# Filter taps of two layers side by side on TensorE, GpSimd's stores moved, own buffers for layer 1's filter pieces

## The reference, cut to what matters

```
hid = sin(freq1 * (z @ w1 + b1))              # z: (256, 33) positions
hid = sin(freq2 * (hid @ w2 + b2))            # (256, 64)
h = (hid @ w3).reshape(256, 2, 512)           # the taps, forward and backward
h = h * exp(-t * abs(decay))                  # the envelope
l1 = sum(abs(h_fwd)) + sum(abs(h_bwd[1:]))    # per channel
filt = concat(h_fwd, 0, reversed h_bwd[1:]) / l1
y = irfft(rfft(u) * rfft(filt))
```

## Time and profile before

| | us |
|---|---|
| median of three runs | 1394.13 |
| lowest, highest | 1393.94, 1396.18 |
| the profiled execution, whole | 1395.68 |
| its span, first to last instruction | 1393.9 |
| PE busy in it | 1356.5 (97%) |
| DVE busy | 780.2 (56%) |
| ACT busy | 547.8 (39%) |
| POOL busy | 193.1 (14%) |

### The profile page before, as it was taken

The page is one execution under the profiler, slowest core; times in us unless marked ns, Lnnn a source line. Parts: engine busy times, 40 slices in busy tenths (PEclk is TensorE's granted clock), DMA queues, the critical chain, the costliest instruction groups (busy, mean ns, idle before and its releaser), DMA issues.

```text
span 1393.9 us, 19649 instructions
## 1 busy us (share of the span) xinstructions
PE 1356.5 (97%) x8084; PEld 1111.0 (80%) x8084; DVE 780.2 (56%) x1127; ACT 547.8 (39%) x847; POOL 193.1 (14%) x179
## 2 busy tenths in 40 slices
PE   7999999999999999999999999999999999999997
PEld 3557756777777887877778888888769999899996
DVE  5555575234548676544223443376866788765663
ACT  5652373332233323433112331244555444553552
POOL 1251000603100152000000002200004404100012
PEclk9999999999999999999999999999999999999999
DMA  9333303444631363345443335324325647455561
GB/s 374 130 108 112 116 1 121 159 166 141 219 124 46 131 246 122 105 148 173 149 152 106 106 105 213 136 81 140 107 75 177 226 137 275 149 189 190 182 195 63
DMA packets 55289, 205.28 MB, mean 147 GB/s; under 512 B 6261, under 2 KB 6645, under 8 KB 53664
## 3 DMA queue, kind: packets, MB, share of 16 engines
q1 hardware_dynamic: 52992, 194.22, 40.1%
q0 software_dynamic: 2208, 9.81, 1.9%
HBM read 200.86 MB, written 3.15 MB: 146 GB/s over the span
## 4 chain that ended last, share of the span: by engine, by line
PE 90%; DVE 4%; ACT 2%; POOL 2%; issue 1%; DMA 1%; SPq 0%; DVEq 0%; ACTq 0%
PE ps L1548 27%; PE ps L1550 26%; PE ps L1549 26%; PE ps L1849 2%; PE ps L1577 2%; PE ps L1860 1%; PE ps L1873 1%; DMA pairs<-in_pairs 1%; PE ps L1945 1%; PE ps L1957 1%; DVE wl L1033 1%; PE ps L1805 1%; PE ps L1602 0%; DVE rstd L1071 0%; ACT wh L720 0%
## 5 line engine op out<-in xcount | busy, mean ns | idle before, releaser
L1548 PE MATMUL ps<-xh,wh 128*128 128x512 f32 (+2 forms) x1392 | 473.3, 340 | 2.7 <-DVE xl L1100 1.4
L1033 DVE TENSOR_TENSOR wl<-raw,wh 128x1024 fp32r<-128x1024 f32 (+2 forms) x272 | 353.8, 1303 | 218.0 <-ACT wh L720 214.9
L1549 PE MATMUL ps<-xl,wh 128*128 128x512 f32 (+2 forms) x1392 | 466.4, 335 | 0.0
L1550 PE MATMUL ps<-xh,wl 128*128 128x512 f32 (+2 forms) x1392 | 466.0, 335 | 0.0
L720 ACT ACTIVATE wh<-raw 128x1024 fp32r<-128x1024 f32 (+2 forms) x272 | 283.6, 1043 | 321.0 <-PE ps L1550 320.2
L1548 PEld LDWEIGHTS ps<-xh,wh 128*128 128x128 f32 (+1 forms) x1392 | 260.4, 187 | 45.2 <-issue 14.3
L1550 PEld LDWEIGHTS ps<-xh,wl 128*128 128x128 f32 (+1 forms) x1392 | 260.6, 187 | 29.1
L1549 PEld LDWEIGHTS ps<-xl,wh 128*128 128x128 f32 (+1 forms) x1392 | 261.5, 188 | 27.9 <-issue 1.0
L1548 PE MATMUL ps<-hid_h,wh 128*128 128x512 f32 (+1 forms) x512 | 172.5, 337 | 0.0
L1549 PE MATMUL ps<-hid_l,wh 128*128 128x512 f32 (+1 forms) x512 | 171.7, 335 | 0.0
L1550 PE MATMUL ps<-hid_h,wl 128*128 128x512 f32 (+1 forms) x512 | 171.6, 335 | 0.0
(11 more groups left out here) (246 smaller groups left out, 1442.9 us busy)
## 6 DMA issues: line engine op xcount, KB each, us to landing
raw<-in_units SPq DMA_DIRECT2D x262, 512.0 KB, 3.3
mod_ring<-in_mod_units SPq DMA_DIRECT2D x49, 512.0 KB, 4.0
gap_hy<-in_mod_units SPq DMA_DIRECT2D x15, 512.0 KB, 5.5
pairs<-in_pairs SPq DMA_DIRECT2D x6, 1024.0 KB, 14.3
gap_relu<-in_mod_units SPq DMA_DIRECT2D x7, 512.0 KB, 4.6
raw<-in_units SPq DMA_DIRECT2D x6, 384.0 KB, 2.9
h<-in_x SPq DMA_DIRECT2D x4, 512.0 KB, 7.9
mod_ring<-in_pairs SPq DMA_DIRECT2D x2, 1024.0 KB, 14.6
```

The source lines that it names most:

```text
L1033: dve.tensor_tensor(wl[:, g % SLOTS, 0:n], raw[:, g % SLOTS, 0:n], wh[:, g % SLOTS, 0:n].bitcast(F), ALU.subtract)\
L1548: pe.matmul(dst, w_h, m_h, start=first, stop=False)
L1549: pe.matmul(dst, w_h, m_l, start=False, stop=False)
L1550: return pe.matmul(dst, w_l, m_h, start=False, stop=last)
```

## The change

- A tap now is two matmuls, one after the other: layer 0's from partitions 0 to 63 into bank 7 and layer 1's from 64 to 127 into bank 6. There are four of these, in wave steps 3 to 6, and none behind the wave. Each waits until both results of the one before are weighted.
- VectorE weights both results, and so needs both envelopes from step 4 on. Its four weightings behind the wave are gone.
- ScalarE makes layer 0's envelope in step 1 instead of 3 and layer 1's in step 4 instead of 6.
- GpSimd's order becomes parts(0), abs_sum(0), parts(1), save(0), abs_sum(1), save(1).
- Layer 1's pieces go to tiles that are free by then (`decay`, `filt_top`, `f_w3`); their copies no longer wait for stores. One semaphore per layer counts the stores, where layer 0 had four.
- TensorE waits for all eight weightings before the first spectrum, since spectra use banks 7 and 6, and later spectra wait for the copy two before in every case.

```diff
+            filt_top = alloc(s, "filt_top", (HY,))
+            filt_out = [[filt0[:, i * HY:(i + 1) * HY] for i in range(4)],
+                        [decay[:, 0:HY], decay[:, HY:], filt_top[:, :], f_w3[:, 0:HY]]]
...
             def filter_parts(f):
                 for tb in range(2):
-                    pool.wait_ge(f_weighted, 4 * f + 2 * tb + 2)
+                    pool.wait_ge(f_weighted, 4 * tb + 3 + f)
...
-                    pool.dma_start(filt_scratch[f, :, i * HY:(i + 1) * HY], filt0[:, i * HY:(i + 1) * HY]).then_inc(f_saved[f][i], 16)
+                    pool.dma_start(filt_scratch[f, :, i * HY:(i + 1) * HY], filt_out[f][i]).then_inc(f_saved[f], 16)
...
             filter_abs_sum(0)
+            filter_parts(1)
             filter_save(0)
-            filter_parts(1)
             filter_abs_sum(1)
...
             def filter_copy(f, i):
-                if f:
-                    act.wait_ge(f_saved[0][i], 16)
                 act.wait_ge(f_spec, 4 * f + i + 1)
-                act.activation(filt0[:, i * HY:(i + 1) * HY], ps[:, 7 - i % 2, :], ACT.Copy).then_inc(f_copied, 1)
+                act.activation(filt_out[f][i], ps[:, 7 - i % 2, :], ACT.Copy).then_inc(f_copied, 1)
...
                 if m == 2:
                     filter_sines(1)
-                elif m == 3:
+                elif m == 1:
                     filter_envelope(0)
-                elif m == 6:
+                elif m == 4:
                     filter_envelope(1)
...
             def filter_weighted(i):
-                f, tb, d = i // 4, i // 2 % 2, i % 2
-                if i % 4 == 0:
+                tb, d = divmod(i, 2)
+                dve.wait_ge(f_taps, i + 1)
+                for f in range(DEPTH):
                     dve.wait_ge(f_env, 2 * f + 2)
-                dve.wait_ge(f_taps, i + 1)
-                src = ps[:, 7 - i % 2, :]
+                    src = ps[:, 7 - f, :]
...
                     latent(i, WAVE_BANKS[i])
-                    for i in range(4, 8):
-                        filter_weighted(i)
                     latent(WAVE, KV1_BANK)
...
             def filter_taps(i):
-                f, tb, d = i // 4, i // 2 % 2, i % 2
-                rows = slice(f * HIDDEN, (f + 1) * HIDDEN)
-                if i >= 2:
-                    pe.wait_ge(f_weighted, i - 1)
-                if i in (4, 5):
-                    pe.wait_ge(f_copied, i - 1)
-                pe.matmul(ps[:, 7 - i % 2, :], f_hid2[rows, tb * 128:(tb + 1) * 128],
-                          f_w3[rows, d * HY:(d + 1) * HY], start=True, stop=True).then_inc(f_taps, 1)
+                tb, d = divmod(i, 2)
+                if i:
+                    pe.wait_ge(f_weighted, 2 * i)
+                for f in range(DEPTH):
+                    rows = slice(f * HIDDEN, (f + 1) * HIDDEN)
+                    mm = pe.matmul(ps[:, 7 - f, :], f_hid2[rows, tb * 128:(tb + 1) * 128],
+                                   f_w3[rows, d * HY:(d + 1) * HY], start=True, stop=True)
+                mm.then_inc(f_taps, 1)
...
             pe.wait_ge(ftab_in_s, 16)
+            pe.wait_ge(f_weighted, 8)
             for i in range(2):
                 filter_spectrum(0, i)
             first_kv()
             for i in range(2, 4):
                 filter_spectrum(0, i)
-            for i in range(4, 8):
-                filter_taps(i)
             key_pe(0)
```

More of the change, by code:

```diff
@@ L425, in backbone @@
         f_env, f_parts, f_abs, f_summed = (sem(n) for n in ("f_env", "f_parts", "f_abs", "f_summed"))
-        f_saved = [sems("f_saved_0", 4), sems("f_saved_1", 1) * 4]
+        f_saved = sems("f_saved")
         f_taps, f_weighted, f_l1, f_l1_ready = sem("f_taps"), sem("f_weighted"), sem("f_l1"), sem("f_l1_ready")
@@ L683, in _ @@
                 pool.wait_ge(y_added[layer], KB)
-                for i in range(4):
-                    pool.wait_ge(f_saved[layer][i], 64 if layer else 16)
+                pool.wait_ge(f_saved[layer], 64)
                 pool.dma_start(ftab[:, :, :], fwd_in).then_inc(tables_loaded, 16)
@@ L1145, in filter_weighted @@
             def filter_weighted(i):
-                f, tb, d = i // 4, i // 2 % 2, i % 2
-                if i % 4 == 0:
+                tb, d = divmod(i, 2)
+                dve.wait_ge(f_taps, i + 1)
+                for f in range(DEPTH):
                     dve.wait_ge(f_env, 2 * f + 2)
-                dve.wait_ge(f_taps, i + 1)
-                e = envelope[:, f, tb, d * HY:(d + 1) * HY]
-                src = ps[:, 7 - i % 2, :]
[L1153 to L1156, removed]
+                    e = envelope[:, f, tb, d * HY:(d + 1) * HY]
+                    src = ps[:, 7 - f, :]
+                    if d:
+                        dve.scalar_tensor_tensor(e, src, not_first[:, tb:tb + 1], e, ALU.mult, ALU.mult).then_inc(f_weighted, 1)
+                    else:
+                        dve.tensor_tensor(e, src, e, ALU.mult).then_inc(f_weighted, 1)
             def filter_l1(f):
@@ L1245, in _ @@
                 if layer == 0:
-                    for i in range(4):
-                        dve.wait_ge(f_saved[DEPTH - 1][i], 64)
+                    for f in range(DEPTH):
+                        dve.wait_ge(f_saved[f], 64)
                 dve.wait_ge(kpe_rotated, layer + 1)
@@ L1693, in filter_spectrum @@
                     pe.wait_ge(f_parts, 4 * f + 4)
-                if i >= 2:
+                if o >= 2:
                     pe.wait_ge(f_copied, o - 1)
```

## The result

The changed kernel takes 1399.56 us (median of 8 runs, 1396.37 to 1401.07) against 1394.26 us for the kernel before (8 runs, 1393.81 to 1396.73): ratio 1.0029, 95% interval 1.0020 to 1.0038. By the medians it is slower by 5.3 us (their quotient is 1.0038), by the recorded ratio by 4.0 us (2.8 to 5.3); 1.0 was forecast, and 1399.56 lies outside the range. The profiled execution took 1401.05 us (span 1399.2).

A forecast was written before the change was run, and what follows sets the result against it. TensorE was taken to bound the wave, GpSimd's chain the stretch behind it up to the last column sums. 0.93 + 0 + 0 + 4 x 0.01 = +1.0 us on 1394.13 gave 1395.1 us, range 1393.0 to 1397.9.

The forecast's parts named there:

- First envelope, +0.93: Wave step 1: the envelope on ScalarE, no longer covered by a tap, delays step 2's matmuls by 0.93 us.
- Taps, 4 x 0.01: Four wave slots: two taps on different row halves run together, adding 0.00 to 0.03 us a slot.
- Rival A: Tap slots: the halves do not run together, each slot grows by 0.82 us, 1398.4 us in all; chance 0.10.
- The four late taps "go", worth nothing: Behind the wave: removing at least 3.3 us of TensorE taps gains nothing, since they lie beside GpSimd's chain.
- Table loads, second envelope, decay: Wave on ScalarE: two added 1.28 us loads, the second envelope at step 4 and its decay load are covered; cost 0.
- D: ScalarE: each table switch takes 1.4 us more than its 1.28, +3.5 us, 1397.7 us; chance 0.02.
- B: Wave: layer 1's decay load lands late; at 13 us it costs 2.6 more, 1397.7 us; chance 0.05.
- GpSimd, 16.8 us: GpSimd's chain to the end of layer 1's sums keeps its 16.8 us; cost 0, the 0.93 passed on.
- C: GpSimd's adds are less disturbed by VectorE's weight remainders, 1.6 us go, 1393.4 us; chance 0.13.
- E: GpSimd: with all four stores behind all sums, 2.19 us would go, 1392.8 us; no separate chance given.
- anything else slower: Catch-all for slower outcomes not named among the forecast's cases; no size, chance 0.02.

The follow-up runs named there:

- fill_end: Changed kernel plus three products of zeros on TensorE ahead of the last column sums; 1394.83 us, ratio 1.0002 to the kernel before.
- env_moved: Kernel before with only the envelopes moved, to wave steps 1 and 4; 1394.90 us, ratio 1.0007 to the kernel before.
- late_fill: Changed kernel plus four products of zeros on TensorE where the four late taps stood; 1395.63 us, ratio 1.0018 to the kernel before.
- stores_last: Changed kernel with all GpSimd stores behind both layers' sums; 1394.18 us, ratio 1.0001 to the kernel before.
- parts_first: Changed kernel with GpSimd's order both layers' parts, then both sums, then stores; 1391.14 us, ratio 0.9979 to the kernel before.
- parts_same_half: Changed kernel with GpSimd doing parts, sums, then stores, and both taps on partitions 0 to 63, layer 1's filter not computed; 1394.64 us, ratio 1.0000.
- env34: Changed kernel with envelopes in wave steps 3 and 4 and an own, early loaded decay tile for layer 1; 1397.44 us, ratio 1.0022.
- b_order: Kernel before with the change's own buffers and GpSimd order, taps as before; 1395.88 us, ratio 1.0007 to the kernel before.
- fill_both: Changed kernel plus three products of zeros ahead of the last column sums and two ahead of wave step 2's turn; 1396.91 us, ratio 1.0017.

## Why the prediction was wrong, point by point

- **First envelope, +0.93.** Right as a stall: six kernels with the envelope in step 1 and no filler there have 30.28 to 30.34 us for the wave against 29.37, so +0.91 to +0.97 (fill_end, env_moved, late_fill, stores_last, parts_first; parts_same_half 32.89 - 3 x 0.85 = 30.34). In the two traces of the change the stall was longer (1.60 and 1.56 instead of 0.85 to 0.88) because ScalarE's copy in step 1 came later against TensorE: at 30.98 and 30.72, where stores_last has 30.09, with the turn at 31.58, 31.37 and 31.46. The addition that leads to it stood behind VectorE's three weight remainders and began at 28.87 and 28.61, against 27.57. Behind the longer stall the clock fell: 5.63 - 4.09 = 1.54 us more. The forecast had no term for that. The late addition goes back to an earlier fall, at 12 to 14 us, before the first instruction that the change moved. The rows are the changed kernel's, then stores_last's:

```profile
12.00:14.00 2.00, 2.00 (x4) 0.86 (x3) 1.97 (x5) 1.86 (x4) 1.06 (x2) 0.50 0.99 412
13.56 4.30 PE L1713 MATMUL ps<-normed,consts 128*128 128x512 f32 x8
12.00:14.00 2.00, 2.00 (x6) 0.73 (x5) 1.97 (x5) 1.98 (x3) 1.06 (x2) 1.00 0.98 410
12.72 3.60 PE L1713 MATMUL ps<-normed,consts 128*128 128x512 f32 x8
```

These eight products end at 17.86 against 16.32, and VectorE's reciprocal, which waits for ScalarE behind them, starts at 18.62 (18.36 in the other trace of the change) against 17.08. Of the fourteen traces only one more, env34's, has the early fall; its addition is late as well (29.02), but no envelope stands in its step 1, and its wave is the old 29.40. Why the early fall came in both traces of the change and in none of the seven other kernels with the envelope in step 1 isn't settled. The change's own eight runs spread over 4.7 us: the five from 1398.76 up have mean clocks of 0.991 to 0.993, the three below 0.994 and 0.995.
- **Taps, 4 x 0.01.** Right: 1.13 us a slot with four instructions, 1.12 before. Rival A is refuted, by the change's trace and by parts_same_half.
- **The four late taps "go", worth nothing.** This is the step that failed most. Their absence saved nothing, as the prediction said, since GpSimd was the bound. But they had also kept TensorE at work until GpSimd was done: its spectra ended at 87.08 + 3.83 = 90.91 and the last sum at 90.98. The prediction itself foresaw "TensorE then waiting for GpSimd ahead of the last column sums" and priced that wait at 0. It was 2.59 us long, and behind it the column sums took 1.72 instead of 1.05 and the sums of squares 7.01 instead of 4.56: 0.67 + 2.45 = 3.1 us on the path. fill_end takes these 3.1 us off this stretch. The taps aren't the only thing that held the gap shut: b_order has all taps and waits 0.96 us, because its parts are late.
- **Table loads, second envelope, decay.** Right, 0. Two loads of 1.28 us were added, and a sine or exponential starts 0.01 to 0.02 us behind a load; D falls. The second absolute value at 47.22 follows the copy at 46.94 directly, without waiting for its load; B falls.
- **GpSimd, 16.8 us.** Right: 76.34 to 91.97 + 1.26 = 93.23, 16.9 us. C's gain didn't come: the last add is down to 1.26 from 2.13, but the two before it are up to 3.63 from 2.63, a remainder of VectorE beside other adds now. The wave's shift is passed on 1:1 here too: from slot 4 to the first sum it is 12.14 us in both traces.
- **E.** The order was read rightly, and stores_last shows what it withholds. The estimate of -2.2 us for it was right for that stretch (34.74 against 36.92). It was reckoned against a kernel without a fall; against the change as it ran, the stretch became 5.43 us shorter.

By size: the steady stretch was forecast at 99.93. From the forecast to 104.37 there are 0.39 us of earlier start (first product of step 2 at 38.23, not 38.62), 1.58 from there to slot 4 (25.97 against 24.39, nearly all the slow step 2), 0.13 of GpSimd's chain and 3.12 behind the last column sums' start: -0.39 + 1.58 + 0.13 + 3.12 = 4.44. Idle time was priced by the wait alone, and of the work taken off TensorE it was only asked what it would save. The range had no mechanism for it: none of the rivals A to E is about TensorE's clock, and "anything else slower" had a chance of 0.02.

## What to carry to other kernels

Work taken off TensorE beside another engine's chain isn't free to remove: if it leaves TensorE standing, look at the granted clock behind the gap, and price what follows at the lower clock too (here 3.1 us behind a gap of 2.6, and 1.7 behind gaps of 0.75 and 0.96). Move the chain that TensorE waits for in the same change (here the stores and layer 1's parts), or fill the gap with products no longer than it is. When an engine's input comes earlier, put the work into that engine's idle time: the early taps let layer 1's parts run in GpSimd's 6.6 us wait, the change didn't use that, and doing so turned +0.3% into -0.2%. One trace is one draw: look for falls of the clock over the whole span before a difference is put down to an edit, and compare distances between instructions that both kernels have.

## What the runs showed of the hardware

- **The granted clock behind idle TensorE.** At the column sums: 2.59 or 2.60 us idle (three traces) were followed by 6.79 to 7.27 us for the sums of squares, 0.96 and 0.75 us by 6.25, 0.29 us or less by 4.56. In the wave, 1.56 and 1.60 us were followed by a fall, 0.85 to 0.88 (six traces) by none. Idle length alone doesn't decide: 0.75 us ahead of the one-column sums and another 0.32 us wait did cost, 0.85 in the wave didn't. Nor does it in one and the same place: ahead of the products of zeros at about 11 us TensorE waited 1.12, 1.33 and 1.35 us in the three traces with the early fall, and 0.65 to 1.70 in the eleven without it. Ahead of layer 1's sums of squares, near 950 us, all fourteen traces wait 0.92 or 0.93 us and then 0.35 or 0.36, and in three (fill_both, stores_last, b_order) the clock falls behind that. What decides is not shown. The Trainium skill (TensorE: Matmul & The Clock Gate, HAM oscillation) names waits of TensorE between bursts of matmuls as what brings the clock down to its lower level; the traces agree in that the falls at the column sums and in the wave stand behind such a wait, but the example there has longer ones, and here gaps of the same length were also followed by no fall.
- **Taps on two halves of the rows.** Two f32 products of 64x128 by 64x512, two instructions each, take 1.13 us on different halves and 1.98 on the same half; one alone takes 1.12. The Trainium skill (TensorE: Matmul & The Clock Gate, Part 3) has matmuls on different row groups start about 4 ns apart; the trace agrees, with 0.01 us more for a slot.
- **GpSimd beside VectorE.** In the changed kernel GpSimd's operations on two 128x512 f32 tiles (adds and subtractions) took 1.26 us at 91.97, with VectorE idle, and 2.25 at 67.47, where VectorE made a weight remainder from 67.35 on, for 1.24 us, and went on with other work. Moving the adds moved which of them was hit; the chain stayed about as long (16.76 and 16.89 us).
